# Output projections of mixer and memory attention as three fp32r products, in a two-layer decoder kernel

## The chip, the cores and the metric

The kernel runs on one core of a Trainium2 chip. The metric is the time of one execution in microseconds of the device; the median of several runs counts. A profiled execution stands beside it, and all rows below are of that one execution. Engines are named as in the profile: PE (TensorE), with its weight loads as PEld, DVE (VectorE), ACT (ScalarE), POOL (GpSimd) and SP, which issues most transfers.

## What is computed

Two layers of a decoder, 256 tokens of width 1024, all in float32:

```
for l in range(2):
    x = layer_norm(alpha * x + hybrid_mixer(x) )        # ... o @ w_out
    x = layer_norm(alpha * x + memory_cross_attention(x, mem))   # ... o @ wo
    f = swiglu(x, ffd_w13, ffd_w2) if l == 0 else moe_swiglu(x, router, w13, w2)
    x = layer_norm(alpha * x + f)
```

The mixer runs three groups of heads over one input projection (differential attention, dilated attention, gated linear attention, GLA) and puts their outputs through `w_out`, 1024x1024. Memory attention has 4 heads of width 256 over 256 memory tokens, with `wq`, `wkv` and `wo`. The second layer's feed-forward has 8 experts; `logits = x @ router` picks the two best for each token, with weights from a softmax over these two logits:

```
top_vals, top_idx = lax.top_k(logits, 2)
gates = one_hot(top_idx) weighted with softmax(top_vals)
out = sum over e of gates[..., e] * swiglu(x, w13[e], w2[e])
```

## The kernel before

**Tiles and panels.** The 256 tokens are two tiles of 128. Dense weights come in panels of 512 output columns, and a panel in two halves of 512 rows, each 128x2048 floats and 1 MB (`DENSE_HALVES`, L68). A layer's panels are, in order, 6 of the input projection, 4 of keys and values of the memory, 2 of `w_out`, 2 of `wq`, 2 of `wo`, and in layer 0 then the feed-forward's. SP loads half after half into five slots of `ring` (`dense`, L429); a slot is refilled when TensorE has read the half in it (`wait_used`, L390).

**Split products.** A half in `SPLIT_HALVES` (L71) is multiplied in fp32r: ScalarE casts it to a high part (`split_high`, L558) in one of four places taken in turn (`high`, L224), VectorE subtracts that from the half and puts the low part into the half's own slot (`split_low`, L885), and TensorE adds three products, high by high, high by low and low by high (`HI_LO`, `gemm`, L1462). The activations are split in the same way while they are turned: TensorE transposes a tile of 128 tokens into two banks of PSUM (`turn_tile`, L1436), ScalarE casts both banks to `x_hi` and VectorE subtracts both into `x_lo` (`turn_split`, L550 and L875). The panels of `w_out`, `wo`, and of keys and values are not split: there TensorE multiplies in plain fp32, each product as two instructions in the profile, and the turned tile is copied, one bank by ScalarE and one by VectorE (`turn`, L540 and L837).

**Order.** There is no planner: each engine has its own program, in order, and semaphores tie them together. So what stands in front of an instruction on its engine holds it up. In each layer, after the heads:

- VectorE takes the mean square of the GLA output of each tile (L1156), GpSimd raises it to -1/2 (L499), VectorE scales and gates (L1162 to L1170) and so releases the turn `mix`, L1738. TensorE then runs both `w_out` panels for tile 0, then both for tile 1 (`gemm_pair`, L1743). VectorE adds each to the residual (`residual`, L863) and takes the layer norm of a tile (`layer_norm`, L850).
- TensorE turns tile 0 of the normed x (`x1`, L1790), runs the query panels for it, turns tile 1, and mixes the query panels of tile 1 with the attention of tile 0 (L1793 to L1800): scores, `cross_turn(0)`, then `turn_q(1)`, which needs VectorE's copy `take_q(1)` (L1214), then `cross_values(0)`. ScalarE takes the exponentials (`cross_exps`, L702) and copies the turned probabilities (`cross_turned`, L709).
- The attention output is turned (`xa`) and the `wo` panels follow, for tile 0 between parts of tile 1's attention (L1804 to L1810), then both for tile 1 (L1813), then x is turned again (`x2`, L1814).

In layer 1, the norm of both tiles and both turns come before the router: 16 products of 8 columns (L1878). VectorE first scales x into the accumulator (L1287), then finds the two best experts by two rounds of maximum, comparison and tie-break (L1294 to L1303). TensorE ranks the tokens of each expert by five small products (L1885 to L1889), VectorE turns ranks into slots (L1308 to L1311) and builds the selection matrix of the first expert (`select`, L1313), TensorE gathers that expert's tokens by it (`gather`, L1900), and the products of the experts begin (`item`, L1945). Expert weights go through seven slots of `ring` (`item_half`, L448), are split into three pairs `w_hi`, `w_lo` (`high`, L581; `low`, L900), and each expert takes 42 halves of 12 products.

Of the kernel before, what the change touches and what calls it, by code (L numbers as in the profile page):

```python
# [74 lines left out]
HIGH_SLOTS = 4  # L75
MOE_PAIRS = F_MOE // N
# [15 lines left out]
def shape_constants():  # L92
# [12 lines left out]
    for v in range(LEVELS):  # L105
# [5 lines left out]
                       np.broadcast_to(i[None, :], (P, P))], 1).astype(np.float32)  # L111
    freq = (THETA ** (-np.arange(0, 2 * ROPE, 2, dtype=np.float32) / np.float32(2 * ROPE))).astype(np.float32)
    e = np.arange(NE, dtype=np.float32)
    rows = np.concatenate([freq, NE - e, e, np.arange(EXTRA, dtype=np.float32)])
# [5 lines left out]
def bass_decoder(nc, a, out):  # L120
    ctx = ExitStack()
    with ctx:
# [16 lines left out]
        ident, before, ones, iota = (square[:, n, :] for n in range(4))  # L139
        rows = sb("rows", [P, ROPE + 2 * NE + EXTRA])  # L140
        freq = rows[:, 0:ROPE]
        desc = rows[:, ROPE:ROPE + NE]
        eid = rows[:, ROPE + NE:ROPE + 2 * NE]
# [7 lines left out]
        lg = sb("lg", [P, 2, T, NE])  # L151
        oh = sb("oh", [P, 2, T, NE])
# [32 lines left out]
        with ExitStack() as scope:  # L185
            def twin(name, shape):
# [18 lines left out]
        x_low = late[:, 0:2048].rearrange("p (c s) -> p c s", c=KC)  # L205
        x_lo = late_r[:, 0:2048].rearrange("p (c s) -> p c s", c=KC)
        pT_cross = dec[:, 0:2, :].rearrange("p v (c s) -> p (v c) s", c=4)
# [16 lines left out]
        high = (ring_r[:, DENSE_SLOTS, :], late_r[:, 8192:10240], late_r[:, 12288:14336],  # L224
                qk_r[:, :, :, :].rearrange("p m n s -> p (m n s)"))
# [76 lines left out]
        logit_psum, chosen_ready, rank2_psum = sem("logit_psum"), sem("chosen_ready"), sem("rank2_psum")  # L302
# [60 lines left out]
        def high_half(l, n, g):  # L363
            return dense_view(high[SPLIT_AT[l, n, g] % HIGH_SLOTS], l, n, g)

# [51 lines left out]
        def _(sp):  # L417
# [47 lines left out]
            for q in range(RAW_SLOTS - 1):  # L465
                if q < DENSE_SLOTS:
                    last = max(i for i in range(len(DENSE_HALVES)) if i % DENSE_SLOTS == q)
                    wait_used(sp, last)
                item_half(q, 0, 0)
# [49 lines left out]
        def _(act):  # L519
# [38 lines left out]
            def split_high(count):  # L558

                for _ in range(count):  # L560
# [4 lines left out]
                    if k >= HIGH_SLOTS:  # L565
                        wait_used(act, HALF_AT[SPLIT_HALVES[k - HIGH_SLOTS]])
                    act.copy(high_half(*name), raw_half(*name)).then_inc(dense_hi, 1)  # L567
# [40 lines left out]
            for l in range(DEPTH):  # L608
# [81 lines left out]
                for t in range(T):  # L690
                    act.wait_ge(gla_out, T * l + t + 1)
                    act.activation(zz[:, t, :], ps[:, 2 + t, 0:CH * CV], ACT.Square).then_inc(gla_square, 1)
# [25 lines left out]
                cross_exps(0)  # L718
                cross_turned(0)
                turn(TURN["q", l], xT, (1,))  # L720
                cross_exps(1)
                turn(TURN["xa", l], xT, (0,))
                cross_turned(1)
                turn(TURN["xa", l], xT, (1,))
                if l == 0:
                    split_high(2)
                    turn_split(TURN["x2", l], (0,))
                    split_high(2)
                else:
                    act.wait_ge(xo_ready, T * (l + 1))  # L730
                    for q in range(SPLIT_SLOTS):
                        high(q, 0, first=True)
                    turn(TURN["x2", l], xT)
# [83 lines left out]
        def _(dve):  # L817
# [57 lines left out]
            def turn_split(m, tiles=range(T)):  # L875

                for t in tiles:
                    for g in range(2):
# [3 lines left out]
                        dve.tensor_tensor(x_lo[at], ps[:, 4 + 2 * t + g, :].rearrange("p (c s) -> p c s", c=4),  # L882
                                          x_hi[at].bitcast(F32), ALU.subtract).then_inc(tp_taken[2 * t + g], 1)

            def split_low(count):  # L885

                for _ in range(count):
# [3 lines left out]
                    dve.tensor_tensor(low_half(*name), raw_half(*name), high_half(*name).bitcast(F32),  # L891
                                      ALU.subtract).then_inc(dense_lo, 1)
# [47 lines left out]
            for l in range(DEPTH):  # L940
# [208 lines left out]
                for s in range(LEVELS + 1):  # L1149
# [3 lines left out]
                    if s == 1:  # L1153
                        dilated_output()
                        dve.sem_inc(dilated_taken, 1)
                for t in range(T):  # L1156
                    dve.wait_ge(gla_square, T * l + t + 1)
                    done(dve.tensor_reduce(var[:, 4 * t:4 * t + 4], zz[:, t, :].rearrange("p (h k) -> p h k", h=CH), AX, ALU.add))
# [54 lines left out]
                cross_max(0)  # L1213
                take_q(1)  # L1214
# [3 lines left out]
                turn(TURN["xa", l], xT, (0,))  # L1218
# [3 lines left out]
                turn(TURN["xa", l], xT, (1,))  # L1222
# [3 lines left out]
                else:  # L1226
                    low(0, 0)
                residual(l, o_p, 0, 1)
                if l == 0:
                    split_low(1)  # L1230
                residual(l, o_p, 1, 1)
                if l == 0:
                    turn_split(TURN["x2", l], (0,))
# [793 lines left out]
```

## Time and profile before

| | |
|---|---|
| median of 3 runs | 1828.35 us (1824.98 to 1829.74) |
| the profiled execution | 1832.96 us, span 1831.1 us, granted TensorE clock 0.98 |
| PE busy | 1743.0 us, 95% |
| DVE, ACT, POOL busy | 1291.2, 983.5, 22.1 us |
| chain that ended last, by engine | PE 90%, DVE 5%, ACT 2%, DMA 1%, issue 1% |
| moved | 465.94 MB, 254 GB/s over the span |

The span runs from the first to the last instruction. Layer 0 fills the first 500 us or so, the mixer and the memory attention of layer 1 the time to about 790, the router to 822, and the eight experts the rest. The chain is found backwards from the last instruction: at each step to what released it, or to the one before it on its engine. In a timeline, the number in brackets is how long the engine had idled before the row, and the arrow what ended that. The clock is a share of 2.4 GHz.

### The profile page before, as it was taken

To read this page: it belongs to the slowest core of one execution; us is meant where nothing else is said; L and a number is where in the kernel's file an instruction comes from. 1 tells how busy PE (TensorE), PEld (TensorE's weight loads), DVE (VectorE), ACT (ScalarE), POOL (GpSimd) and SP (SyncE) were. 2 spreads that over 40 slices of the span, in tenths; PEclk is the share of its full clock that TensorE was granted. 3 is DMA by queue.
4 is the path that set the end of the run, shared out by engine and by line. 5 is a ranking of instruction groups with operands and counts; after the bars stand their busy time and mean duration, and the time that the engine had idled before them with its cause. 6 is when DMAs were issued, how large, how long until landed. Compare 5 with 4: busy or idle time off the path is not lost.

```text
span 1831.1 us, 21349 instructions
## 1 busy us (share of the span) xinstructions
PE 1743.0 (95%) x7850; PEld 1354.0 (74%) x7850; DVE 1291.2 (71%) x1209; ACT 983.5 (54%) x871; POOL 22.1 (1%) x32
## 2 busy tenths in 40 slices
PE   7989998998989999879999999999999999999996
PEld 6846565887777465657888888888888888888884
DVE  4465525554454655248989889899899898898996
ACT  4353222434333422117767777677777776777772
POOL 0001000000000010000000000000000000000000
PEclk9999999999999999979999999999999999999998
DMA  8512432645634233278999999999999999999991
GB/s 290 183 63 83 154 116 96 225 150 177 217 138 146 93 115 108 76 253 297 358 344 368 371 346 362 353 358 366 338 363 370 347 359 359 349 369 343 364 369 43
DMA packets 206470, 465.94 MB, mean 254 GB/s; under 512 B 11952, under 2 KB 14544, under 8 KB 206416
## 3 DMA queue, kind: packets, MB, share of 16 engines
q1 hardware_dynamic: 200880, 463.76, 70.4%
q10 hardware_dynamic: 5536, 1.45, 0.3%
q8 instruction: 35, 0.57, 0.1%
q14 instruction: 19, 0.16, 0.0%
HBM read 464.13 MB, written 1.05 MB: 254 GB/s over the span
## 4 chain that ended last, share of the span: by engine, by line
PE 90%; DVE 5%; ACT 2%; DMA 1%; issue 1%; ACTq 0%; DVEq 0%; SPq 0%
PE ps L1483 22%; PE ps L1927 16%; PE ps L1929 16%; PE ps L1928 16%; PE ps L1513 5%; PE ps L1849 3%; PE ps L1907 2%; PE ps L1916 1%; DVE w_lo L903 1%; PE ps L1444 1%; PE ps L1639 1%; PE ps L1775 1%; PE ps L1757 1%; PE ps L1694 1%; PE ps L1596 1%
## 5 line engine op out<-in xcount | busy, mean ns | idle before, releaser
L903 DVE TENSOR_TENSOR w_lo<-ring,w_hi 128x2048 fp32r<-128x2048 f32 x336 | 768.0, 2290 | 120.4 <-ACT w_hi L586 117.6
L586 ACT CAST w_hi<-ring 128x2048 fp32r<-128x2048 f32 x336 | 642.0, 1911 | 279.9 <-PE ps L1929 265.0
L1927 PE MATMUL ps<-w_hi,xe_hi 128*128 128x512 f32 x896 | 353.2, 394 | 3.2 <-DVE w_lo L903 1.8
L1929 PE MATMUL ps<-w_hi,xe_lo 128*128 128x512 f32 x896 | 349.3, 390 | 0.0
L1928 PE MATMUL ps<-w_lo,xe_hi 128*128 128x512 f32 x896 | 348.7, 389 | 0.0
L1927 PEld LDWEIGHTS ps<-w_hi,xe_hi 128*128 128x128 f32 x896 | 168.3, 188 | 38.7 <-DVE w_lo L903 2.8
L1929 PEld LDWEIGHTS ps<-w_hi,xe_lo 128*128 128x128 f32 x896 | 168.2, 188 | 35.7
L1928 PEld LDWEIGHTS ps<-w_lo,xe_hi 128*128 128x128 f32 x896 | 168.4, 188 | 33.8
L1927 PE MATMUL ps<-w_hi,he_hi 128*128 128x512 f32 x448 | 178.2, 398 | 0.0
L1929 PE MATMUL ps<-w_hi,he_lo 128*128 128x512 f32 x448 | 174.8, 390 | 0.0
L1928 PE MATMUL ps<-w_lo,he_hi 128*128 128x512 f32 x448 | 174.4, 389 | 0.0
L1483 PE MATMUL ps<-ring_r,xT_r 128*128 128x512 f32 (+1 forms) x560 | 148.7, 396 | 11.7 <-DVE late_r L882 6.8
L1483 PEld LDWEIGHTS ps<-ring_r,xT_r 128*128 128x128 f32 x560 | 105.0, 193 | 35.6 <-DVE late_r L882 7.6
L1483 PE MATMUL ps<-ring,xT 128*128 128x512 f32 x256 | 115.4, 609 | 9.4 <-ACT xT L545 6.3
L1513 PE MATMUL ps<-ring,memT 128*128 128x512 f32 x256 | 121.2, 604 | 0.0
L1483 PEld LDWEIGHTS ps<-ring,xT 128*128 128x128 f32 x256 | 49.2, 195 | 69.5 <-issue 62.6
L1929 PEld LDWEIGHTS ps<-w_hi,he_lo 128*128 128x128 f32 x448 | 84.1, 188 | 18.0
L1928 PEld LDWEIGHTS ps<-w_lo,he_hi 128*128 128x128 f32 x448 | 84.3, 188 | 16.2
L567 ACT CAST late_r<-ring 128x2048 fp32r<-128x2048 f32 (+1 forms) x34 | 63.1, 1858 | 61.6 <-DMA ring<-in_xa_wq_dram 17.1
L1927 PEld LDWEIGHTS ps<-w_hi,he_hi 128*128 128x128 f32 x448 | 84.2, 188 | 16.1
L891 DVE TENSOR_TENSOR ring_r<-ring,late_r 128x2048 fp32r<-128x2048 f32 (+1 forms) x34 | 75.5, 2227 | 29.2 <-ACT late_r L567 28.3
L1513 PEld LDWEIGHTS ps<-ring,memT 128*128 128x128 f32 x256 | 44.9, 192 | 41.4 <-issue 40.4
(264 smaller groups left out, 1778.4 us busy)
## 6 DMA issues: line engine op xcount, KB each, us to landing
ring<-in_moe_w_dram SPq DMA_DIRECT2D x336, 1024.0 KB, 5.2
ring<-in_ffd_w_dram SPq DMA_DIRECT2D x31, 1024.0 KB, 5.1
ring<-in_w_in_dram SPq DMA_DIRECT2D x24, 1024.0 KB, 5.2
ring<-in_xa_wkv_dram SPq DMA_DIRECT2D x16, 1024.0 KB, 5.0
ring<-in_w_out_dram SPq DMA_DIRECT2D x8, 1024.0 KB, 5.0
ring<-in_xa_wq_dram SPq DMA_DIRECT2D x8, 1024.0 KB, 5.0
ring<-in_xa_wo_dram SPq DMA_DIRECT2D x8, 1024.0 KB, 5.0
ring<-in_ffd_w_dram SPq DMA_DIRECT2D x4, 512.0 KB, 3.5
```

The costliest lines, as they stand in the source:

```text
L567: act.copy(high_half(*name), raw_half(*name)).then_inc(dense_hi, 1)
L586: act.copy(w_hi[:, q % SPLIT_SLOTS, :], ring[:, q % RAW_SLOTS, :]).then_inc(hi_ready, 1)
L891: dve.tensor_tensor(low_half(*name), raw_half(*name), high_half(*name).bitcast(F32), ALU.subtract).then_inc(dense_lo, 1)
L903: dve.tensor_tensor(w_lo[:, q % SPLIT_SLOTS, :], ring[:, q % RAW_SLOTS, :], w_hi[:, q % SPLIT_SLOTS, :].bitcast(F32), ALU.subtract).then_i ...
L1444: ins = pe.transpose(ps[:, 4 + b, c * P:(c + 1) * P], src[:, t, k * P:(k + 1) * P], ident)
L1483: ins = pe.matmul(ps[:, b, 0:w], lhs[:, 4 * g + c, t * P:(t + 1) * P], rhs[:, c, :], start=(g == 0 and m == 0 and c == 0), stop=(g == 1 an ...
L1513: ins = pe.matmul(ps[:, piece_bank(i), :], memT[:, k, t * P:(t + 1) * P], raw_half(l, IN_P + n, g)[:, c, :], start=(k == 0), stop=(k == KC ...
L1849: ins = pe.matmul(ps[:, t + 2 * col, :], (h_hi, h_lo)[p][:, k, t * P:(t + 1) * P], weights[q][:, c, col * N:(col + 1) * N], start=(k == 0 ...
L1907: ins = pe.matmul(ps[:, 6 + b, c * P:(c + 1) * P], x[:, t, k * P:(k + 1) * P], sel[:, t, :], start=(t == 0), stop=(t == T - 1))
L1927: pe.matmul(ps[:, bank, :], x_hi, hi[:, c, cols], start=first, stop=False)
L1928: pe.matmul(ps[:, bank, :], x_hi, lo[:, c, cols], start=False, stop=False)
L1929: return pe.matmul(ps[:, bank, :], x_lo, hi[:, c, cols], start=False, stop=last)
```

## The change

The panels of `w_out` and `wo` join the split halves; only those of keys and values stay in plain fp32. So 16 more halves get a high and a low part, the turns `mix` and `xa` become split turns (the low part of `xa` goes to `xa_lo`, over the turned keys), and `gemm` has only the three products. The high parts now have places by stage (`high_homes`), since the four old ones are in use there, and ScalarE waits for the half that was last in a place (`HIGH_BEFORE`). Two of the places lie in two pieces, so that views of four dimensions are taken (`as_high`). The squares of the GLA output move to `gla_sq`, out of a place of the high parts.

The order changes as well: the turn of `x1` tile 0 stands between the two `w_out` panels of tile 1, the turn of `x2` tile 0 between the two `wo` panels of tile 1. The router's products for tile 0 come before tile 1's turn. The two best experts are found by comparing all pairs of an expert's logits, the scaling of x is moved behind the first gather, the count of tokens per expert has a semaphore of its own and its two products come after the gather, slots count from 1, and the first expert product waits for one of the gathered banks instead of both. SP waits for the last half whose high part was in the sixth slot before it loads an expert half there.

```diff
-SPLIT_HALVES = [(l, n, g) for l, n, g in DENSE_HALVES
-                if n < IN_P or n >= MIX_PANELS or 0 <= n - (IN_P + KV_P + OUT_P) < Q_P]
+SPLIT_HALVES = [(l, n, g) for l, n, g in DENSE_HALVES if not IN_P <= n < IN_P + KV_P]
...
+def high_homes():
...
+            stage = (n - IN_P - KV_P) // 2
+            at = 2 * ((n - IN_P - KV_P) % 2) + g
+            homes[l, n, g] = (("h_qk", "dec_early", "tr", "dec_late"),
+                              ("ring", "o_tok", "qk", "dec_early"),
+                              ("dec_late", "h_gate", "ring", "qk"))[stage][at]
```

On ScalarE:

```diff
                 act.activation(h[:, :, C_G:C_RANK], h[:, :, C_G:C_RANK], ACT.Silu).then_inc(gate_silu, 1)
+                split_high(1)
                 take_piece(l, 5)
+                act.wait_ge(level_ready, (GSTEPS - 1) * l + 4)
+                split_high(1)
                 take_piece(l, 6)
...
+                act.wait_ge(level_ready, (GSTEPS - 1) * (l + 1))
+                split_high(1)
                 turn(TURN["k", l], kT)
                 take_piece(l, 7)
-                turn(TURN["mix", l], xT)
-
-                act.wait_ge(tp_ready[3], TURN["mix", l] + 1)
-                split_high(2)
+                turn_split(TURN["mix", l])
+                split_high(1)
+
+                split_high(1)
                 turn_split(TURN["x1", l], (0,))
-                split_high(2)
+                split_high(3)
...
                 cross_exps(0)
+                split_high(2)
                 cross_turned(0)
                 turn(TURN["q", l], xT, (1,))
+                split_high(1)
                 cross_exps(1)
-                turn(TURN["xa", l], xT, (0,))
+                turn_split(TURN["xa", l], (0,))
+                split_high(1)
                 cross_turned(1)
-                turn(TURN["xa", l], xT, (1,))
+                turn_split(TURN["xa", l], (1,))
```

On VectorE:

```diff
+                split_low(1)
                 for t in range(T):
                     dve.wait_ge(gla_square, T * l + t + 1)
...
+                split_low(1)
                 for t in range(T):
                     dve.wait_ge(rstd_ready, POWERS * l + t + 2)
...
-                turn(TURN["mix", l], xT)
+                for t in range(T):
+                    turn_split(TURN["mix", l], (t,))
+                    split_low(1)
 
                 out_p = IN_P + KV_P
                 residual(l, out_p, 0, 0)
+                split_low(1)
                 residual(l, out_p, 1, 0)
                 layer_norm(3 * l, x, 0)
-                split_low(1)
                 residual(l, out_p, 0, 1)
+                turn_split(TURN["x1", l], (0,))
                 split_low(1)
                 residual(l, out_p, 1, 1)
-                turn_split(TURN["x1", l], (0,))
                 split_low(2)
...
                 cross_max(0)
+                split_low(2)
                 take_q(1)
                 turn(TURN["q", l], xT, (1,))
                 cross_output(0)
                 cross_max(1)
-                turn(TURN["xa", l], xT, (0,))
+                turn_split(TURN["xa", l], (0,), xa_lo)
+                split_low(2)
                 residual(l, o_p, 0, 0)
                 cross_output(1)
                 residual(l, o_p, 1, 0)
-                turn(TURN["xa", l], xT, (1,))
+                turn_split(TURN["xa", l], (1,), xa_lo)
                 layer_norm(3 * l + 1, x, 0)
...
+            dve.wait_ge(logit_psum, T)
             done(dve.tensor_copy(lg[:, 0], ps[:, 4, 0:T * NE].rearrange("p (t e) -> p t e", t=T)))
+            done(dve.tensor_tensor(above[:, 0], lg[:, 0].unsqueeze(2).to_broadcast(pairs),
+                                   lg[:, 0].unsqueeze(3).to_broadcast(pairs), ALU.subtract))
+            done(dve.scalar_tensor_tensor(above[:, 1], above[:, 0], 0.0, earlier.unsqueeze(1).to_broadcast(pairs),
+                                          ALU.is_equal, ALU.mult))
+            done(dve.scalar_tensor_tensor(above[:, 0], above[:, 0], 0.0, above[:, 1], ALU.is_gt, ALU.add))
+            done(dve.tensor_reduce(order[:, :, :], above[:, 0], AX, ALU.add))
+            done(dve.tensor_scalar(chosen[:, :, :], order[:, :, :], 2.0, None, ALU.is_lt))
```

On TensorE:

```diff
-                for t in range(T):
-                    turned(TURN["mix", l], t)
-                    gemm_pair(l, IN_P + KV_P, t)
+                turned(TURN["mix", l], 0)
+                gemm_pair(l, IN_P + KV_P, 0)
+                turned(TURN["mix", l], 1)
+                gemm(l, IN_P + KV_P, (1,))
+                pe.wait_ge(ln_done, T * 3 * l + 1)
+                turn_tile(TURN["x1", l], x, 0)
+                gemm(l, IN_P + KV_P + 1, (1,))
...
                 turned(TURN["xa", l], 1)
-                gemm_pair(l, o_p, 1)
+                gemm(l, o_p, (1,))
                 turn_x("x2", 3 * l + 1, 0)
+                gemm(l, o_p + 1, (1,))
...
+                    router(0)
                     turn_x("x2", 3 * l + 1, 1)
                     turned(TURN["x2", l], 1)
...
+                    router(1)
```

In layer 1, VectorE now copies its half of the turn `x2` tile 0 ahead of the first expert half's subtraction and of the last residual, and subtracts the second expert half ahead of the turn of tile 1.

## Rows read from the trace of the kernel before

**Rows 1.** Windows: us, busy us per engine (x instructions), clock, DMA share, GB/s.
```profile
1082.00:1208.00 126.00, 126.00 (x588) 104.82 (x587) 111.63 (x70) 91.17 (x63) 0.00 (x0) 1.00 0.99 358
```

**Rows 2.** Waits of PE from 830 to 1800 us: us in total, times, longest.
```profile
PE ps L1927 <- DVE w_lo L903: 1.8, 4, 0.5
```

**Rows 3.** The chain in order of time: start us, us, what.
```profile
182.28 3.44 PE ps L1513 x8
...
187.53 27.72 PE ps L1483 x64
218.22 12.94 PE ps L1483 x48
...
301.30 11.41 PE ps L1483 x48
...
372.90 22.31 PE ps L1483 x96
```

**Rows 4.** Timeline, PE behind three waits: start us, us, instructions, [idle before].
```profile
218.22 3.44 PE L1483 MATMUL ps<-ring_r,xT_r 128*128 128x512 f32 x8 [2.12 <-DVE late_r L882]
...
261.93 8.83 PE L1483 MATMUL ps<-ring,xT 128*128 128x512 f32 x16 [3.14 <-ACT xT L545]
...
711.79 1.18 PE L1483 MATMUL ps<-qk_r,xT_r 128*128 128x512 f32 x4 [2.11 <-DVE late_r L882]
```

**Rows 5.** Groups by line: busy us, mean ns of one, then idle before.
```profile
L903 DVE TENSOR_TENSOR w_lo<-ring,w_hi 128x2048 fp32r<-128x2048 f32 x336 | 768.0, 2290 | 120.4 <-ACT w_hi L586 117.6
L586 ACT CAST w_hi<-ring 128x2048 fp32r<-128x2048 f32 x336 | 642.0, 1911 | 279.9 <-PE ps L1929 265.0 <-DMA ring<-in_moe_w_dram 13.0 <-issue 1.2
...
L882 DVE TENSOR_TENSOR late_r<-ps,xT_r 128x512 fp32r<-128x512 f32 x20 | 13.0, 687 | 33.3 <-ACT xT_r L555 33.2
...
L555 ACT CAST xT_r<-ps 128x512 fp32r<-128x512 f32 x20 | 10.8, 588 | 23.2 <-PE ps L1444 22.9
```

**Rows 6.** Timeline of DVE at the end of layer 0's mixer.
```profile
177.56 0.55 DVE L1158 TENSOR_REDUCE var<-late 128x4 f32<-128x384 f32 x1 [3.73 <-ACT late L692]
...
183.50 0.17 DVE L847 TENSOR_SCALAR var<-var 128x4 f32<-128x4 f32 x1
...
185.71 0.56 DVE L1169 TENSOR_TENSOR late<-late,h 128x384 f32<-128x384 f32 x1
...
205.05 1.28 DVE L860 SCALAR_TENSOR_TENSOR x<-x,rstd,ln_gb 128x1024 f32<-128x1024 f32 x1
```

**Rows 7.** Timeline of layer 0's memory attention, tile 0.
```profile
246.46 0.21 ACT L705 ACTIVATION_READ_ACCUMULATOR late<-ps,nmax 128x1 f32 x1
...
248.80 0.69 DVE L832 COPY h<-ps 128x512 f32<-128x512 f32 x1 [4.15 <-PE ps L1483]
...
250.74 3.72 PE L1775 MATMUL ps<-late 128*128 128x256 f32 x16
```

**Rows 8.** Window of 2 us behind the wait before 261.93.
```profile
264.00:266.00 2.00, 2.00 (x3) 0.68 (x3) 0.00 (x0) 0.00 (x0) 0.00 (x0) 0.50 0.00 0
```

**Rows 9.** Timeline from layer 1's last panel to the first expert product.
```profile
780.07 11.77 SPq L457 DMA_DIRECT2D ring<-in_moe_w_dram  x6
...
790.97 0.69 DVE L869 SCALAR_TENSOR_TENSOR x<-x,ps 128x512 f32<-128x512 f32 x1
...
799.42 6.97 PE L1880 MATMUL ps<-w_router,xT 128*128 128x8 f32 x32 [0.87 <-DVE xT L842]
...
806.42 1.23 DVE L1287 TENSOR_SCALAR accum<-x 128x2048 f32<-128x2048 f32 x1 [2.75 <-PE ps L1880]
...
810.25 0.18 DVE L1303 TENSOR_TENSOR chosen<-oh 128x16 f32<-128x16 f32 x1
...
812.95 0.17 DVE L1308 TENSOR_TENSOR rtmp<-ps,chosen 128x16 f32<-128x16 f32 x1 [2.26 <-PE ps L1889]
...
813.89 0.48 DVE L1316 TENSOR_SCALAR sel<-square,slot 128x128 f32<-128x128 f32 x2
...
822.04 0.47 PE L1927 MATMUL ps<-w_hi,xe_hi 128*128 128x512 f32 x1 [1.45 <-DVE xe_lo L1330]
```

More of the change, by code:

```diff
@@ L75 @@
 HIGH_SLOTS = 4
+def high_homes():
+    homes = {}
+    turn = 0
+    for l, n, g in SPLIT_HALVES:
+        if n < IN_P or n >= MIX_PANELS:
+            if (n, g) == (MIX_PANELS, 0):
+                homes[l, n, g] = "tr"
+                turn = 0
+                continue
+            homes[l, n, g] = ("o_tok", "dec_late", "ring", "qk")[turn % HIGH_SLOTS]
+            turn += 1
+        else:
+            stage = (n - IN_P - KV_P) // 2
[3 more added lines that the diff above has]
+                              ("dec_late", "h_gate", "ring", "qk"))[stage][at]
+    return homes
+HIGH_HOME = high_homes()
+HIGH_BEFORE = {name: max((m for m in SPLIT_HALVES[:i] if HIGH_HOME[m] == HIGH_HOME[name]), default=None)
+               for i, name in enumerate(SPLIT_HALVES)}
 MOE_PAIRS = F_MOE // N
@@ L138, in bass_decoder @@
         square = sb("square", [P, 4, P])
-        ident, before, ones, iota = (square[:, n, :] for n in range(4))
-        rows = sb("rows", [P, ROPE + 2 * NE + EXTRA])
+        ident, before, ones, place = (square[:, n, :] for n in range(4))
+        rows = sb("rows", [P, ROPE + NE + NE * NE])
         freq = rows[:, 0:ROPE]
-        desc = rows[:, ROPE:ROPE + NE]
-        eid = rows[:, ROPE + NE:ROPE + 2 * NE]
+        eid = rows[:, ROPE:ROPE + NE]
+        earlier = rows[:, ROPE + NE:].rearrange("p (e f) -> p e f", e=NE)
         w_router = sb("w_router", [P, KC, NE])
@@ L151, in bass_decoder @@
         lg = sb("lg", [P, 2, T, NE])
+        above = sb("above", [P, 2, T, NE, NE])
+        order = sb("order", [P, T, NE])
         oh = sb("oh", [P, 2, T, NE])
@@ L467, in _ @@
                     last = max(i for i in range(len(DENSE_HALVES)) if i % DENSE_SLOTS == q)
-                    wait_used(sp, last)
+                else:
+                    last = max(HALF_AT[name] for name in SPLIT_HALVES if HIGH_HOME[name] == "ring")
+                wait_used(sp, last)
                 item_half(q, 0, 0)
@@ L873, in _, with turn_split @@
             x_turns, dense_splits = [0], [0]
[L875 removed]
+            def turn_split(m, tiles=range(T), low_into=x_lo):
                 for t in tiles:
@@ L1237, in _ @@
                 else:
-                    turn(TURN["x2", l], xT, (0,))
                     layer_norm(3 * l + 1, x, 1)
+                    low(1, 0)
                     turn(TURN["x2", l], xT, (1,))
@@ L1407, in item @@
                         for t in range(T):
-                            ins = dve.tensor_scalar(back[:, t, :], iota, slot[:, t, bass.ds(i, 1)], None, ALU.is_equal)
+                            ins = dve.tensor_scalar(back[:, t, :], place, slot[:, t, bass.ds(i, 1)], None, ALU.is_equal)
                         ins.then_inc(back_ready, 1)
@@ L1873, in _, with router @@
                 else:
+                    def router(t):
+                        for k in range(KC):
+                            ins = pe.matmul(ps[:, 4, t * NE:(t + 1) * NE], xT[:, k, t * P:(t + 1) * P],
+                                            w_router[:, k, :], start=(k == 0), stop=(k == KC - 1))
+                        ins.then_inc(logit_psum, 1)
+                    router(0)
                     turn_x("x2", 3 * l + 1, 1)
                     turned(TURN["x2", l], 1)
-            for t in range(T):
-                for k in range(KC):
-                    ins = pe.matmul(ps[:, 4, t * NE:(t + 1) * NE], xT[:, k, t * P:(t + 1) * P], w_router[:, k, :],
-                                    start=(k == 0), stop=(k == KC - 1))
-            ins.then_inc(logit_psum, 1)
+                    router(1)
             pe.wait_ge(chosen_ready, 1)
@@ L1945, in item @@
             def item(i, first=False):
-                if first:
-                    for b in range(2):
-                        pe.wait_ge(misc_taken[b], 1)
                 for q in range(4 * MOE_PAIRS):
                     n, g, r = q // 4, q // 2 % 2, q % 2
+                    if first and q < 2:
+                        pe.wait_ge(misc_taken[q], 1)
                     taken = (g_taken, he_ready)[g]
```

121 lines of the change are left out of this document (62 added, 59 removed).

## The prediction

> **What bounds the kernel now.** I read first the chain that ended last, by engine: nearly all of it is TensorE's. Then the stages by window: from 830 us on, while the eight experts stream, TensorE is busy in all of a 126 us window at a granted clock of 1.00, and VectorE and ScalarE have room [rows 1]; in 970 us it waits 1.8 us in all for another engine [rows 2]. So the expert part is a block as long as TensorE's work, and what starts it earlier ends it earlier. All that counts of this change is when the first expert product issues, 822.04 before [rows 9]. The rest of the reading is the chain in order of time between 180 and 822 us [rows 3], then the engines' timelines where the edits lie.
>
> **The products.** One output projection is 32 products of 128x512, which in plain fp32 are 64 instructions and 27.72 us at 187.53 [rows 3]. In three fp32r passes it is 96 instructions; the feed-forward shows 96 of that shape in 22.31 us without a gap at 372.90 [rows 3]. That is 5.4 us less per projection, 21.6 us for four.
>
> **The splits.** Each of 16 weight halves now gets a cast on ScalarE and a subtraction on VectorE. Rows of the same shape: 1911 and 2290 ns [rows 5]. That is 30.6 and 36.6 us of engine time, and only their place in the engines' queues says what they cost.
>
> **Mixer projection (twice).** Of the four subtractions, the first falls into VectorE's 3.73 us idle before the GLA variance [rows 6] and costs nothing; without that cover 2.29. The second stands between the second variance and the two scalings that release the mixer's turn. Nothing is idle there: the variance ends at 183.67, the scalings at 186.27 [rows 6], so they end 2.29 later, at 188.56. VectorE, which only copied its half of the turn before, now also subtracts both blocks of tile 0, 2 x 0.687 [rows 5], so the first product starts at about 190.05 instead of 187.53 [rows 3]: **+2.5**. The third and fourth subtraction and the first query half end at 192.2, 195.9 and 199.8, each ahead of the product that reads it. Tile 0's two panels end at 201.2 and tile 1's first at 206.8; tile 0's layer norm ended 4.94 after its panels (206.33 [rows 6] after 187.53 + 13.86), so now at 206.2. So the turn of x1 tile 0, now between tile 1's two panels, finds its input ready, and its cast and subtraction run beside the last panel. The 2.12 and 2.11 us that TensorE waited there go away [rows 4]: -2.1 in each layer. If the norm came later it would stall TensorE between the panels; the margin is 0.6. The other query halves are loaded as their slots fall free, panel by panel as before; I find their subtractions ready 1 to 4 us ahead of the products.
>
> In layer 0 the 48 products behind that wait took 12.94 us; 48 behind an equal wait in the feed-forward 11.41 [rows 3]. The difference, 1.5, is the low clock, and goes with the wait. Sum: layer 0 -5.4 - 2.1 - 1.5 + 2.5 = **-6.5**; layer 1, with no low clock there, **-5.0**.
>
> **Memory attention (twice).** Here the order bites. ScalarE ends tile 0's exponentials at 246.67 [rows 7] and now casts two halves before it copies the turned probabilities; VectorE subtracts these halves before it takes the query panel. Casts end at 248.6 and 250.5, subtractions at 250.9 and 253.2, and only then comes the copy that stood at 248.80 to 249.49 [rows 7]; it ends at 253.9. TensorE's next instructions, the turn of query tile 1, need that copy, and behind them in its queue stand the value products: 250.74 before [rows 7], now 254.85, **+4.1**. Then tile 0's turned output was copied by one instruction per engine; now it takes two casts in a row and a subtraction behind each. Cast 0.588 + subtraction 0.687 [rows 5] plus the hop: **+1.4** ahead of the first panel, and +0.65 at tile 1, where the second engine's copy used to end late. The other two subtractions lie beside that panel's products and cost nothing; without cover 4.6. The products give -5.4.
>
> The new wait, from 249.5 to 253.9, is longer than the 3.14 before 261.93, after which 16 instructions took 8.83 [rows 4] instead of a quarter of 27.72, 6.93, at a granted clock of 0.50, the 1.2 GHz level [rows 8]. So one fall costs 1.5 to 1.9. Bounds for the new wait: nothing (the clock stays), or two such prices; I take one, **+1.9**, as the wait is above both that showed a fall. The fall at 261.93 I leave as it was. Up to the end of the projection: +4.1 + 1.4 + 0.65 + 1.9 - 5.4 = +2.65.
>
> Layer 0: the turn of x2 tile 0 moves ahead of the last panel, which removes a wait like those of the mixer, 2.1: **+0.55**. Layer 1: the last panel ends 0.87 later for that turn. The residual behind it no longer waits for an expert half's subtraction (at 790.97 it ran 0.6 after its panel [rows 9]), nor the norm for a copy of 0.69: -1.3. So the norm ends 2.2 later.
>
> **Router.** Behind the norm the half-turn and its copy are as before (the expert subtraction put ahead of the copy lies beside the turn, +0.1). Half of the 32 router instructions, 6.97 us [rows 9], runs while tile 1's norm is awaited: -3.5. The scaling of x, 1.23 at 806.42 [rows 9], is moved behind: -1.1, as its end overlapped the next operation. From there to the choice 14 operations end at 810.43 [rows 9], 0.205 each; the new chain has 6, of which four see 128 elements per partition. No row has these operations: 0.205 to 0.39 each; I take 0.3, so 1.6 for 2.9: -1.3. Three ranking products for the five that VectorE awaited 2.26: -0.9. Slots: 0.94 from 812.95 to 813.89 [rows 9] becomes one operation: -0.7. The first expert product had waited 1.45 [rows 9] for two gathered banks; it now waits for one, with two count products ahead: -0.6. Sum -8.1, and layer 1's part 2.2 + 0.1 - 8.1 = **-5.8**.
>
> The scaling of x behind the gather, and the operations on the count, hide behind the first expert half's 12 products. The expert loads start when the projection's slots fall free at 780.07 [rows 9], so they move with it, and as many halves are loaded or under way at the first product as before. SP's queue gets no new wait but the one for the sixth slot, which is free by the time that the fourth is.
>
> **Sum.** -6.5 + 0.55 - 5.0 - 5.8 = -16.75 on a span of 1831.1, whose execution took 1832.96. The median of the runs, 1828.35, is 4.6 lower; I take the difference off the median: **1811.6 us**. A measurement of this kernel can tell about 0.3% (5.5 us) from no change.
>
> **Rivals.**
> - *The clock stays up* in memory attention, at the old and the new wait: 1.9 less in each of four places, 1804. For: the wait of 2.11 before 711.79 passed without a fall (4 instructions in 1.18 us behind it), while behind the like wait before 218.22 8 took 3.44 [rows 4]. Against: the waits here are longer. Chance 0.18.
> - *The clock falls more often.* The mixer's tail gets new waits between 185.72, when TensorE ends the key and value pieces [rows 3], and 190.05; priced 1.5 per layer, and two prices at each new wait in memory attention: +3.0 + 3.8, 1818.4. For: 0.50 in 264 to 266 [rows 8]. Against: 711.79. Chance 0.17. The Trainium skill, "TensorE: Matmul & The Clock Gate", section "HAM oscillation — how this bites in real kernels", says that idle gaps between bursts of matmuls put the engine back to the low clock, and that each burst then pays anew; by it this rival would be the likeliest, and the trace agrees at 261.93 but not at 711.79.
> - *Transport decides the expert part.* The DMA engines are 0.99 busy there at 358 GB/s [rows 1]. If loads rather than products set the pace, the end moves with the first load alone: -6.5 + 0.55 - 5.0 + 2.65 = -8.3, 1820. Against: TensorE waits 1.8 us in 970 [rows 2]. Chance 0.06.
> - *Slower.* VectorE is in order, and each subtraction can stand ahead of a copy that TensorE awaits. I count six of 16 on the path. Each further one costs 2.29; from the eighth further one the gain of 16.75 is gone; all ten give +6.2, 1834.5. For: the query copy shows how it goes. Against: VectorE had idled 3.73 and 4.15 us ahead of two rows there [rows 6, 7]. Chance 0.06.
>
> The forecast has 0.53, and its own range is 1806 to 1817; with the clock's two rivals and the transport it is 1804 to 1821. Faster by over 0.3%: 0.86; within: 0.08; slower: 0.06.
>
> **What would show it.** Right: 96 instructions in about 22.5 us for a projection; no wait before the query products and layer 0's feed-forward; a new wait of some 4 us before query tile 1's turn, with VectorE's subtractions just ahead; 16 router instructions early; the first expert product near 805. Wrong, if the value products start without that wait, if the granted clock is 1.00 through memory attention (then 1804), if expert products wait for loads, or if subtractions stand before the residuals.

## The result, and the profile after

The changed kernel takes 1816.88 us (median of 5 runs, 1814.60 to 1819.08) beside 1829.47 for the kernel before (5 runs): a ratio of 0.993, with a 95% interval of 0.9913 to 0.9947, or 12.6 us less. In a later set of runs it took 1815.70 beside 1828.71: 13.0 less, 0.9924 (0.9907 to 0.9941). The forecast was 1811.6, in a range of 1804 to 1821. Its profiled execution took 1814.82 us, its span is 1813.0: 18.1 less than the profiled execution of before, and so more than the medians differ. Part of the explanation below is where that difference comes from. Two executions far outside the rest, of 2910 and 6374 us, are left out of the medians and ranges of the experiments below.

The page of the changed kernel, TensorE's share of the busy time first, then the chain that ended last:

```profile
PE 1722.1 (95%) x7978; PEld 1378.6 (76%) x7978; DVE 1331.1 (73%) x1229; ACT 1017.5 (56%) x895; POOL 22.2 (1%) x32
...
PE 88%; DVE 6%; ACT 2%; issue 1%; DMA 1%; DVEq 0%; ACTq 0%; SPq 0%
```

TensorE is busy 21 us less, VectorE 40 and ScalarE 34 us more, and VectorE's share of the chain grows from 5% to 6%. Where, the chain in order of time tells. First some links of the kernel before that were not needed for the prediction (the turn of the keys that both kernels reach at about the same time, the first query products of tile 1 in both layers, a weight transfer, the turn of the keys in layer 1):

```profile
180.53 1.75 PE ps L1444 x16
...
233.90 5.83 PE ps L1483 x24
...
423.53 7.08 DMA ring<-in_ffd_w_dram
...
674.10 1.75 PE ps L1444 x16
...
725.91 5.84 PE ps L1483 x24
```

The chain of the changed kernel at the same places, with the projection's products, the value products and the `wo` panels between them:

```profile
180.90 1.76 PE ps L1507 x16
...
190.52 16.95 PE ps L1542 x72
207.48 0.87 PE ps L1507 x8
208.35 16.71 PE ps L1542 x72
...
227.80 5.83 PE ps L1542 x24
...
249.52 5.28 PE ps L1837 x16
...
263.65 7.20 PE ps L1542 x24
...
283.74 7.37 PE ps L1542 x24
...
419.46 4.79 DMA ring<-in_ffd_w_dram
...
666.73 1.76 PE ps L1507 x16
...
713.75 5.83 PE ps L1542 x24
...
733.50 1.19 PE ps L1507 x8
734.69 5.04 PE ps L1837 x16
```

In the mixer, 96 products of `w_out` and 48 of the query panel run from 190.52 to 225.06 with one turn between them and no wait: 33.66 us for 144 is 22.4 for a projection. The waits before 218.22 and 711.79 [rows 4] are gone. In memory attention, three stretches show products at half speed. The timeline of TensorE there, and from the last norm to the first expert product:

```profile
247.55 1.97 PE L1507 MATMUL ps<-square,h 128*128 128x128 f32 x8 [4.04 <-DVE h L888]
...
263.65 2.04 PE L1542 MATMUL ps<-late_r,xT_r 128*128 128x512 f32 x4 [4.52 <-DVE late_r L938]
...
283.74 1.99 PE L1542 MATMUL ps<-late_r,xT_r 128*128 128x512 f32 x4 [2.11 <-DVE late_r L938]
...
787.44 1.97 PE L1507 MATMUL ps<-square,x 128*128 128x128 f32 x8 [3.38 <-DVEq L917]
...
804.38 0.49 PE L1993 MATMUL ps<-w_hi,xe_hi 128*128 128x512 f32 x1
```

The first wait is new, the second was 3.14 [rows 4], the third was 1.51, and in the kernel before the 32 instructions behind it ran at full speed:

```profile
284.34 13.97 PE L1483 MATMUL ps<-ring,xT 128*128 128x512 f32 x32 [1.51 <-issue]
```

Behind each of the three the clock now falls; one window of 2 us (busy time per engine, then the granted clock):

```profile
250.00:252.00 2.00, 2.00 (x6) 1.56 (x6) 0.34 (x2) 1.09 (x1) 0.00 (x0) 0.50 0.01 2
```

And VectorE's timeline, at the end of the mixer and ahead of the first of these waits:

```profile
174.35 2.29 DVE L947 TENSOR_TENSOR ring_r<-ring,h_r 128x2048 fp32r<-128x2048 f32 x1
...
184.19 2.33 DVE L947 TENSOR_TENSOR ring_r<-ring,late_r 128x2048 fp32r<-128x2048 f32 x1
186.44 0.55 DVE L1223 TENSOR_TENSOR late<-ps,rstd 128x384 f32<-128x384 f32 x1
...
242.40 2.29 DVE L947 TENSOR_TENSOR ring_r<-ring,late_r 128x2048 fp32r<-128x2048 f32 x1 [3.86 <-ACT late_r L611]
244.61 2.29 DVE L947 TENSOR_TENSOR ring_r<-ring,h_r 128x2048 fp32r<-128x2048 f32 x1
246.81 0.68 DVE L888 COPY h<-ps 128x512 f32<-128x512 f32 x1
```

These rows show the same thing twice: a weight subtraction that nobody awaits yet stands ahead of the operation that TensorE awaits (the scalings at 186.44, the query copy at 246.81).

### The profile page after: what moved, and what is told of

Read it like the earlier page. It is cut to its first block, busy times and chain, and to the rows that moved or that the text cites. A ratio compares the mean times of both kernels' runs of the same rounds, so it can differ in the third digit from the quotient of the medians.

```text
span 1813.0 us, 21662 instructions
## 1 busy us (share of the span) xinstructions
PE 1722.1 (95%) x7978; PEld 1378.6 (76%) x7978; DVE 1331.1 (73%) x1229; ACT 1017.5 (56%) x895; POOL 22.2 (1%) x32
## 4 chain that ended last, share of the span: by engine, by line
PE 88%; DVE 6%; ACT 2%; issue 1%; DMA 1%; DVEq 0%; ACTq 0%; SPq 0%
PE ps L1542 21%; PE ps L1993 16%; PE ps L1995 16%; PE ps L1994 16%; PE ps L1571 4%; PE ps L1911 3%; PE ps L1970 2%; PE ps L1979 1%; DVE w_lo L959 1%; PE ps L1837 1%; PE ps L1507 1%; PE ps L1697 1%; PE ps L1819 1%; PE ps L1752 1%; DVE ring_r L947 1%
## 5 line engine op out<-in xcount | busy, mean ns | idle before, releaser
L1542 PE MATMUL ps<-ring_r,xT_r 128*128 128x512 f32 (+1 forms) x704 | 188.2, 397 | 10.2 <-DVE late_r L938 10.2
L1542 PEld LDWEIGHTS ps<-ring_r,xT_r 128*128 128x128 f32 x704 | 133.2, 193 | 40.8 <-DVE late_r L938 11.0
L947 DVE TENSOR_TENSOR ring_r<-ring,late_r 128x2048 fp32r<-128x2048 f32 (+1 forms) x43 | 96.2, 2242 | 36.3 <-ACT late_r L611 35.4
L611 ACT CAST late_r<-ring 128x2048 fp32r<-128x2048 f32 (+1 forms) x43 | 80.3, 1869 | 40.8 <-PE ps L1911 14.6
L1542 PE MATMUL ps<-late_r,xT_r 128*128 128x512 f32 (+1 forms) x296 | 83.6, 406 | 19.8 <-DVE late_r L938 14.9
L1542 PEld LDWEIGHTS ps<-late_r,xT_r 128*128 128x128 f32 x296 | 56.5, 197 | 33.1 <-DVE late_r L938 15.9
L1542 PE MATMUL ps<-late_r 128*128 128x512 f32 (+1 forms) x296 | 79.6, 391 | 0.0
```

Source lines behind the costliest of these rows:

```text
L611: act.copy(high_half(*name), as_high(raw_half(*name), *name)).then_inc(dense_hi, 1)
L947: dve.tensor_tensor(as_high(low_half(*name), *name), as_high(raw_half(*name), *name), high_half(*name).bitcast(F32), ALU.subtract).then_in ...
L1542: ins = pe.matmul(ps[:, b, 0:w], acts[p][:, 4 * g + c, t * P:(t + 1) * P], weights, start=(g == 0 and m == 0 and c == 0), stop=(g == 1 and ...
```

## The experiments

Each kernel was timed in five rounds beside the kernel before (1828.48 in the first four, 1829.26 in the next four, 1828.71 in the last two). The baseline of those that edit the changed kernel is 1816.9, 1815.7 in its second set.

**The query copy first.**

```diff
                 cross_max(0)
-                split_low(2)
                 take_q(1)
                 turn(TURN["q", l], xT, (1,))
+                split_low(2)
```

> Edit: of the changed kernel, only VectorE's order in memory attention: the two weight subtractions go from ahead of the query copy to behind query tile 1's turn. Theory: they cost the 4.04 us that TensorE waits there (all but some 0.5 that ScalarE's two casts hold back the turned probabilities) and the low clock behind it (turn 1.97 and value products 5.28 in place of 0.87 and 3.45, 2.9 us): 6.4 less per layer, 12.9 in all, 1816.9 to 1804.0, and a granted clock of 1.00 at the value products. Rival 1, the clock falls for another reason: 3.5 less per layer, 1809.9, value products still near 5.3. Rival 2, the subtractions only move and hold up tile 0's attention output instead: near 1816.9, with a longer wait ahead of the output projection.

Measured: 1806.42 (1803.40 to 1807.36), 10.5 less. TensorE's timeline:

```profile
245.08 3.72 PE L1837 MATMUL ps<-late 128*128 128x256 f32 x16 [0.61 <-ACT late L760]
...
257.64 2.05 PE L1542 MATMUL ps<-late_r,xT_r 128*128 128x512 f32 x4 [4.51 <-DVE late_r L938]
```

The wait of 4.04 is gone, 0.61 for ScalarE's copy is left, and the 16 value products take 3.72 again. The second wait, 4.51, is as long as it was: it follows the value products wherever they stand. The panel behind it takes 8.24 in place of 7.20 in this execution, which is 1.0 of what is missing from the 12.9. Another 1.0 is layer 1's low clock, which in the changed kernel cost 1.9 there (1.19 + 5.04 at 733.50 against 0.87 + 3.45) and not the 2.9 of layer 0. Both rivals are out.

**Work in the wait, the wait kept.**

```diff
                 cross_turn(0)
+                for _ in range(8):
+                    pe.matmul(ps[:, 0, 0:S], kT[:, 0, 0:P], kT[:, 0, :], start=True, stop=True)
                 turn_q(1)
```

> Edit: of the changed kernel, eight products of 128x256 that nobody reads stand in TensorE's queue ahead of the wait for the query copy (some 3.5 us at the full clock, inside the wait of 4.04). Theory: the wait is VectorE's and stays (the value products follow the copy as before), but TensorE is not idle, so the clock stays at 1.00 there: turn and value products take 4.3 in place of 7.2, 2.9 less per layer, 1816.9 to 1811.1. Rival, the clock falls for something other than the idle time: 1816.9, or up to 1821 if the eight run at the low clock and end behind the copy.

Measured: 1812.16 (1811.61 to 1812.91), 4.7 less than the changed kernel's first set and 3.5 less than its second.

```profile
244.08 3.62 PE L1862 MATMUL ps<-late 128*128 128x256 f32 x16
248.28 1.09 PE L1507 MATMUL ps<-square,h 128*128 128x128 f32 x8 [0.58 <-DVE h L888]
249.21 3.62 PE L1837 MATMUL ps<-late 128*128 128x256 f32 x16
```

The query copy ends as late as before, the kernel has more work, and it is faster: with eight needless products (16 instructions) in the wait, the turn takes 1.09 and not 1.97 and the value products 3.62 and not 5.49 on the timeline. So the low clock there comes from TensorE's idle time, and its price, 2.7 by these two rows, comes on top of the wait. The granted clock is 1.00 from 250 to 252 us, where the changed kernel had 0.50. The gain is less than the 5.8 of the theory mainly because that counted layer 0's price in both layers: 2.9 and 1.9 are 4.8. The Trainium skill, "TensorE: Matmul & The Clock Gate", section "HAM oscillation — how this bites in real kernels", tells of a kernel whose bursts of matmuls start at the low clock after each idle gap between them; this pair of runs agrees.

**The turns behind both panels again.** TensorE's part of the edit:

```diff
-                gemm(l, IN_P + KV_P, (1,))
+                gemm_pair(l, IN_P + KV_P, 1)
                 pe.wait_ge(ln_done, T * 3 * l + 1)
                 turn_tile(TURN["x1", l], x, 0)
-                gemm(l, IN_P + KV_P + 1, (1,))
...
-                gemm(l, o_p, (1,))
+                gemm_pair(l, o_p, 1)
                 turn_x("x2", 3 * l + 1, 0)
-                gemm(l, o_p + 1, (1,))
```

> Edit: of the changed kernel, tile 0's turns of x1 and x2 go back behind both of tile 1's panels (with their casts and subtractions, and one weight cast ahead of them, as in the kernel before). Theory: a wait of 2.1 us comes back at x1 in both layers and at x2 in layer 0, some with a low clock behind it (1.5), and 0 to 0.7 at x2 in layer 1: 6.3 to 10 more, 1823 to 1827. Rival, the turn's own 0.87 between the panels and the later residual had eaten the gain: 1817 to 1819.

Measured: 1829.35 (1827.67 to 1832.46), 12.5 to 13.7 more: no faster than the kernel before (0.9993 to 1.0015). More than the theory had, mostly because the waits that come back are longer than those of before: 3.15 and 3.01 ahead of the query products, 3.23 ahead of layer 0's feed-forward, the last two with a low clock behind them (48 products in 12.94). The chain in front of the query products that issue at 217.50, behind a wait of 3.15 where [rows 4] had 2.12:

```profile
205.17 5.14 DMA ring<-in_xa_wq_dram
210.33 1.92 ACT late_r L611
212.35 2.29 DVE ring_r L947
214.64 0.61 DVE x L925
```

VectorE's residual stands behind the subtraction of a query half, which waits for its cast, and that for its transfer. Before, the same transfer landed at 209.91 and TensorE's products ended at 215.25, so the residual followed the products; with the products 5.4 us shorter, the transfer is last. The moved turn takes its place in front of that subtraction. Without the moved turns the rest of the change gains nothing that can be measured. The new router is part of that rest, and alone it gains 8.1 (next experiment). If the parts add up, which no run tried, the four projections as fp32r products would by themselves cost some 8 us without the moved turns, and gain some 5 with them (12.6 to 13.0, less 8.1).

**The router alone, on the kernel before.** The diff is the router's part of the change (selection by pairs, router by tile, slots, counts, scaling behind the gather), and nothing else.

> Edit: the kernel before with the new router alone (router by tile, rank by comparison of all pairs, one slot operation, count products and the scaling of x behind the gather). Theory: TensorE's work sets the expert part, so the whole 8.1 us that the steps from the last norm to the first expert product lose is seen at the end: 1829.5 to 1821.4, first expert product near 814. Rival, transport: the expert loads start when they did (780.07), so the end stays, 1829, and the first products wait for weights.

Measured: 1820.41 (1817.02 to 1821.66), 8.1 less, 0.9953 (0.9940 to 0.9966). The issue of the expert loads, and the first expert product:

```profile
775.54 11.77 SPq L461 DMA_DIRECT2D ring<-in_moe_w_dram  x6
...
809.58 0.48 PE L1936 MATMUL ps<-w_hi,xe_hi 128*128 128x512 f32 x1
```

From the loads to the first product it is 34.0 us here and was 42.0 [rows 9]; from that product to the end of the span 1008.9 and 1009.1. The loads did not move against the work ahead of them (they start 3.70 us behind the `wo` products of tile 1 in both kernels), the products did, and the end came with the products. The rival of transport is out.

This profile is also a second look at the two layers as they were before, and two links of its chain differ from the first:

```profile
219.20 11.41 PE ps L1488 x48
...
423.00 4.85 DMA ring<-in_ffd_w_dram
```

The 48 products behind the wait took 12.94 before [rows 3], and the transfer 7.08. The code of these stretches and the data are the same, so both belong to the one execution that the prediction was worked out from. The 12.94 is the exception: of the six waits of 2.11 or 2.12 us in these two profiles, ahead of the query products of either layer and of layer 0's feed-forward, only that one was followed by a low clock.

**Three more orders, one by one.** In the first, VectorE subtracts tile 1's turned attention output before a residual that stood ahead of it:

```diff
                 cross_output(1)
+                turn_split(TURN["xa", l], (1,), xa_lo)
                 residual(l, o_p, 1, 0)
-                turn_split(TURN["xa", l], (1,), xa_lo)
```

> Edit: of the changed kernel, VectorE's two subtractions of the attention output's turn, tile 1, go ahead of the residual of the second panel, tile 0, which stands before them. Theory: they then end with ScalarE's second cast and not 0.6 us later, TensorE waits 1.5 in place of 2.11 ahead of the output projection's tile 1, as before the change, and as then the clock stays up behind it (5.6 for the panel in place of 7.4): 2.3 to 2.4 less per layer, 1816.9 to 1812.2. Rival, the clock falls behind 1.5 too: 0.6 less per layer, 1815.7.

Measured: 1813.23 (1811.36 to 1814.98), 2.5 to 3.7 less, between the two and nearer to the theory. The rows decide:

```profile
285.09 1.17 PE L1542 MATMUL ps<-late_r,xT_r 128*128 128x512 f32 x4 [1.61 <-DVE late_r L938]
```

The wait is 1.61 in both layers, and four products take 1.17 and not 1.99, as do those behind them: the clock stays up. This execution also has a low clock in layer 1's mixer, where nothing was edited: in its heads (below), and at the first `w_out` products (four in 2.05 at 675.90), behind a wait of 1.61 for the mixer's turn.

In the second, the mixer's scalings go ahead of the second weight subtraction:

```diff
-                split_low(1)
                 for t in range(T):
                     dve.wait_ge(rstd_ready, POWERS * l + t + 2)
...
-                for t in range(T):
-                    turn_split(TURN["mix", l], (t,))
-                    split_low(1)
+                turn_split(TURN["mix", l], (0,))
+                split_low(3)
+                turn_split(TURN["mix", l], (1,))
```

> Edit: of the changed kernel, the mixer's second weight subtraction goes behind the two scalings that release the mixer's turn and behind tile 0's split turn. Theory: the scalings end 2.3 earlier and the first product starts 2.1 to 2.3 earlier (near 188.3 in place of 190.5 in layer 0), nothing else waits: 4.4 less in all, 1812.5. Rival, the second and third weight half are then late and TensorE waits for them inside the panels: 1816 to 1818.

Measured: 1811.99 (1810.27 to 1812.69), 3.7 to 4.9 less, as the theory has it. The 72 instructions of the first panels take 16.95 as they did, so no half is late. Counted from the keys' turn, the first product comes 1.8 earlier (189.28 - 181.46 against 190.52 - 180.90), a little less than 2.1, since TensorE now waits 0.89 for the split turn itself.

In the third, ScalarE casts before it takes exponentials:

```diff
+                turn_split(TURN["xa", l], (0,))
                 cross_exps(1)
-                turn_split(TURN["xa", l], (0,))
                 split_high(1)
```

> Edit: of the changed kernel, ScalarE casts tile 0's turned attention output before tile 1's exponentials and not behind them. Theory: the wait of 4.52 us ahead of the output projection is those exponentials (some 1.8), one stage of VectorE's maximum and the split turn; it falls to some 2.0, 2.5 less per layer, and where the clock then stays up (7.20 to 5.58 for the panel) another 1.6: 1812 without, 1808.7 with it. Rival, tile 1's exponentials come too late for its turn of probabilities, and TensorE waits there instead: 1817.

Measured: 1808.15 (1807.81 to 1808.55), 7.6 to 8.7 less. TensorE's timeline at the second and the third wait:

```profile
261.62 1.17 PE L1542 MATMUL ps<-late_r,xT_r 128*128 128x512 f32 x4 [2.13 <-DVE late_r L938]
...
280.33 1.64 PE L1542 MATMUL ps<-late_r,xT_r 128*128 128x512 f32 x4 [2.11 <-DVE late_r L938]
```

The wait fell from 4.52 to 2.13 in each layer, and the clock stayed up behind it, but not behind the third wait, which is as long.

**All of them.** The query copy, with one weight subtraction ahead of the query turn and one behind it, and the three orders above.

> Edit: the changed kernel with the three edits above, and the query copy ahead of the weight subtractions, one of which stands before query tile 1's turn and one behind it; of the two casts that stood ahead of the turned probabilities one goes behind. Theory: the places add up, since each is a wait of its own on TensorE's path: query 10.5 to 11.5, third wait 4.7, scalings 4.4, attention output 4.9 to 8.2, 1816.9 to 1788 to 1792. Rival, one wait hides behind another or the clock falls elsewhere in their stead: 1796 to 1804.

Measured: 1790.39 (1788.76 to 1792.70), a ratio of 0.978 (0.9761 to 0.9799). The four single gains, taken from 1816.3, the mean of the changed kernel's two medians, are 9.9, 3.1, 4.3 and 8.1: together 25.4, and 1790.9. So they are separate waits, and none hid another by more than the runs can tell.

**Two more turns moved as the change moved its two.** TensorE's part of the edit:

```diff
-                cross_scores(1)
+                cross_scores(1, range(XH // 2))
                 turn_xa(0)
+                cross_scores(1, range(XH // 2, XH))
...
-                gemm(l, o_p + 1, (0,), range(KC // 2, KC))
+                gemm(l, o_p + 1, (0,), range(KC // 2, KC), range(2))
                 turn_xa(1)
+                gemm(l, o_p + 1, (0,), range(KC // 2, KC), range(2, 3))
```

> Edit: the kernel with the four orders, and TensorE's turns of the attention output moved as the change moved those of x1 and x2: tile 0's between the halves of query tile 1's scores (its subtractions right behind the scores, ahead of the maximum), tile 1's between the second and third pass of the second panel's last half. Theory: the waits of 2.13 and 1.61 ahead of the output projection shrink by 1.3 and 1.1 in each layer, 4.8 less than the 1790.4 of the four orders, 1785.6, and 1784 where the clock no longer falls. Rival, the turn now waits for VectorE's scaled output inside the scores, or tile 1's maximum and exponentials come late: 1790.

Measured: 1784.86 (1783.86 to 1787.08), 0.9755 (0.9737 to 0.9773), the fastest here. Its waits ahead of the `wo` panels:

```profile
255.08 1.17 PE L1546 MATMUL ps<-late_r,xT_r 128*128 128x512 f32 x4 [1.43 <-DVE late_r L939]
...
272.35 1.15 PE L1546 MATMUL ps<-late_r,xT_r 128*128 128x512 f32 x4 [0.68 <-DVE late_r L939]
```

They shrank by 0.7 and 0.9 where 1.3 and 1.1 were expected; in layer 1 the panel at full clock gave most of the rest (5.81 for 7.35 in the four orders).

**The changed kernel again.**

> Edit: none, the changed kernel again beside the others. Both theories: 1815 to 1818, the w2 weights' wait near 4.8 (in the one profile of the kernel before it was 7.08, in the router alone, whose layer 0 is that of before, 4.85); if it comes out near 7 here, the 2.3 are chance in either kernel.

Measured: 1815.70 (1813.98 to 1817.77). The transfer ahead of the w2 products takes 4.89, and so it is the 7.08 of the one profile of before that stands alone: in the eleven other profiles it takes 4.79 to 5.08.

## Why the prediction was right, and where not

**Direction, place and most sizes were right.** The rows of the two profiled executions give each part, from one turn or product to the next:

| part | forecast | measured | from |
|---|---|---|---|
| mixer, layer 0 | -6.5 | -6.5 | 233.90 - 180.53; 227.80 - 180.90 |
| memory attention, layer 0, to the first feed-forward product | +0.55 | +2.2 | 301.30 [rows 3] - 233.90; 297.42 - 227.80 |
| feed-forward, layer 1's heads | 0 | -3.5 | 674.10 - 301.30; 666.73 - 297.42 |
| mixer, layer 1 | -5.0 | -4.8 | 725.91 - 674.10; 713.75 - 666.73 |
| memory attention and router, layer 1 | -5.8 | -5.5 | 822.04 [rows 9] - 725.91; 804.38 - 713.75 |

With 0.4 at either end this is the 18.1 between the spans. Two of the near hits are partly luck. The first row holds for the execution that the forecast was read from, with a low clock of 1.5 us that the second profile of the same code lacks. The last row is the sum of two misses; the norm of tile 1 ends, before and after, with

```profile
795.00 1.30 DVE x L860
...
786.04 1.30 DVE x L916
```

so up to there it is 3.2 more (forecast 2.2), and from there to the first expert product 8.7 less (forecast 8.0).

- *Products.* 5.4 less per projection: measured 27.72 [rows 3] to 22.4, as forecast.
- *The second mixer subtraction, +2.5.* The first product came at 190.52 (forecast 190.05, with 0.4 of offset in this execution). That the subtraction is the cause is shown by the kernel with the scalings first. The first subtraction fell into idle time, as said.
- *The turn of x1 between the panels.* No wait, as forecast, and it carries more than its 2.1: put back, the waits are 3.0 to 3.2, since the trace of before priced it with the slower products in front.
- *The query copy, +4.1.* Measured 4.04, shown by putting the copy first. *The split turns, +1.4 and +0.65:* the second wait grew from 3.14 to 4.52, the third from 1.51 to 2.11.
- *The router, -8.1.* 8.1 alone, on the kernel before, by the medians.

**What failed is the clock.** The forecast had one new fall per layer at 1.9, and took one old one away (1.5). Measured, per layer:

- At the new wait the price was 2.9 in layer 0: 1.97 + 5.28 for the turn and the value products, against 0.87 and 3.45 at full speed. In layer 1 it was 1.9 (1.19 + 5.04), as forecast.
- A fall behind the third wait was not forecast at all: 7.37 in place of 5.82, 1.6 us. The step that failed is "+0.65 at tile 1": its wait was priced right and the clock behind it was left out. This is nearly all of layer 0's miss in memory attention (+2.2 for +0.55). The kernel that shortens this wait to 1.61 shows the fall gone. Over all profiles, this wait at 2.11 or 2.12 us was followed by a low clock in 13 of 14 places (both layers in seven profiles), and at 1.51 to 1.61 in none of 8 (both layers in the two profiles of the old layers, in this kernel and in the four orders).
- The 1.5 taken off in the mixer was one execution's chance; in the second profile of that code the 48 products took 11.41.

**And the frame was one execution.** The sum was worked out from an execution 4.6 us above the median and taken off the median. Two items of that execution's own were in what the spans show: the 2.3 of the transfer (not in the sum) and the 1.5 of the clock (in it). Without these the 18.1 are 14.3, nearer to the 12.6 and 13.0 of the medians. A third may be the low clock in layer 1's mixer heads, some 1.1 us, which the two profiles of the old layers have and the two of the changed kernel lack; but it comes in 3 of the 8 edited kernels as well, so I count it as open.

**The rivals.** The changed kernel lies at 1815.7 to 1816.9, between the forecast and the rival in which the clock falls more often (1818.4). That rival had its falls in the mixer's tail, where none came in the changed kernel's two profiles (four products take 1.16 at 190.52 after the waits there), and had the right kind in memory attention. The Trainium skill's rule, page and section as above, was the better guide in memory attention than the row of 711.79 on which its chance was cut: there all eight waits of 4.0 or 4.5 us in these two profiles were followed by a low clock, and three of the four of 2.11. That the clock stays up, the transport and the slower case are out by the traces, the last with this remark: its mechanism, a subtraction ahead of an awaited operation, cost microseconds only in the two places that were counted. The prediction also named a subtraction ahead of a residual as a sign of being wrong, and there is one: an expert half's, 780.40 to 782.69, ahead of layer 1's last residual, which it holds up by some 0.2 us.

## What to carry to other kernels

When a copy becomes a split, list for each engine what its in-order queue now holds ahead of the operation that the bounding engine awaits; work that is needed later goes behind it. Here four such swaps and two turns moved into other work were worth another 31 us, more than twice the change itself. Price a wait on the bounding engine with the slower stretch behind it, and look at more than one execution before a stretch that varies is added or taken off.

## What the hardware showed that was not expected

- *The same wait in the same code may or may not cost the clock.* Ahead of the third `wo` stretch of layer 1, the changed kernel waited 2.11 in both of its profiles; in the first, four products behind it took 2.05 (768.58), in the second:

```profile
770.16 1.16 PE L1542 MATMUL ps<-late_r,xT_r 128*128 128x512 f32 x4 [2.11 <-DVE late_r L938]
```

  In the four orders a wait of 2.13 was followed by a fall in layer 1 (7.35 for 24 instructions) and by none in layer 0 (5.81). The length of the wait alone does not decide either. With the turns put back, the longer of two waits for the same products left the clock up:

```profile
217.50 2.10 PE L1542 MATMUL ps<-ring_r,xT_r 128*128 128x512 f32 x8 [3.15 <-DVE late_r L938]
...
711.11 3.65 PE L1542 MATMUL ps<-ring_r,xT_r 128*128 128x512 f32 x8 [3.01 <-DVE late_r L938]
```

  What decides was not tried, beyond that work in the wait keeps the clock.
- *Needless work on the bounding engine made the kernel faster*: 16 instructions of 0.22 us each per layer, 3.5 to 4.7 us less in all.
